# A two-block transformer kernel: weight splits begun at projection steps only, key rotation behind its tile, norm broadcasts behind the projection

## The reference, cut to what matters

```
block 1:  xn = rmsnorm(x)
          q_a,k_a,v_a, q_b,f_b,i_b,og_b, g_a,g_b = split(xn @ w_in)      # 9 x 1024 columns
          y_a = attention(rope(q_a), rope(k_a), v_a; 16 heads of 64, causal) @ w_br_attn
          y_b = hgrn2(q_b, f_b, i_b, og_b; 8 heads of 128, norm per head) @ w_br_hgrn
          h = x + (sigmoid(g_a)*y_a + sigmoid(g_b)*y_b) @ w_out
          h = h + cross_attention(rmsnorm(h), rmsnorm(mem); 4 heads of 256) @ wo
          h = h + (silu(u)*v) @ w_ffn_out,  u,v = split(rmsnorm(h) @ w_ffn_in)  # hidden 2816
          x = rmsnorm(h)
block 2, layer 0 (adaLN from c; 512 tokens, 8 heads):
          q,k,v,z = split(h @ a_w_in);  q,k = rope(q), rope(k)           # image tokens only
          o = softmax(q1 k1) v - lam * softmax(q2 k2) v
          o = rmsnorm(o, subln_g) per head * (1 - lam_init)
          x = x + gate * rmsnorm((o * silu(z)) @ w_out)
block 2, layer 1: grouped-query attention (8 query, 2 key heads of 128), norm of q and k, rope,
          the same frame
```

## Time and profile before

| | before |
|---|---|
| median of 3 runs (lowest to highest) | 1512.51 us (1512.04 to 1514.78) |
| profiled execution: its own time | 1509.61 us |
| its span, first to last instruction | 1507.8 us |
| TensorE (PE) busy | 1281.3 us, 85% |
| PE weight load busy (beside PE) | 1118.7 us, 74% |
| VectorE (DVE) busy | 809.2 us, 54% |
| ScalarE (ACT) busy | 591.9 us, 39% |
| GpSimd (POOL) busy | 53.6 us, 4% |
| granted TensorE clock, mean over the span | 0.908 of full |
| DMA | 170.80 MB, 113 GB/s |

### The profile page before, as it was taken

The page is one execution under the profiler, slowest core; times in us unless marked ns, Lnnn a source line. Parts: engine busy times, 40 slices in busy tenths (PEclk is TensorE's granted clock), DMA queues, the critical chain, the costliest instruction groups (busy, mean ns, idle before and its releaser), DMA issues.

```text
span 1507.8 us, 22059 instructions
## 1 busy us (share of the span) xinstructions
PE 1281.3 (85%) x8336; PEld 1118.7 (74%) x8336; DVE 809.2 (54%) x1600; ACT 591.9 (39%) x1053; POOL 53.6 (4%) x57
## 2 busy tenths in 40 slices
PE   3899998987966798999999989988888779696886
PEld 3899887887965797988888877765555557585485
DVE  3565544558736855555664435554454352654653
ACT  3674345342221243433333334544433233343442
POOL 0000000002112000000000000000000000010000
PEclk9899999998987899999999979999888879588998
DMA  5254443332211252387846711121111012022020
GB/s 227 95 177 155 141 141 112 126 126 85 98 70 56 99 188 81 130 303 286 310 172 232 273 42 67 61 70 42 42 42 42 28 42 84 28 71 70 1 85 29
DMA packets 46809, 170.80 MB, mean 113 GB/s; under 512 B 5200, under 2 KB 5840, under 8 KB 46064
## 3 DMA queue, kind: packets, MB, share of 16 engines
q1 hardware_dynamic: 46080, 165.58, 31.2%
q0 software_dynamic: 624, 3.80, 0.7%
HBM read 168.31 MB, written 1.05 MB: 112 GB/s over the span
## 4 chain that ended last, share of the span: by engine, by line
PE 62%; issue 16%; DVE 12%; ACT 4%; POOL 0%; ACTq 0%; DVEq 0%; POOLq 0%
PE lin L1003 14%; PE lin L1004 13%; PE lin L1005 13%; PE sum_bank L1059 4%; PE lin L1017 3%; PE lin L1019 2%; PE lin L1018 2%; DVE w_lo L1400 2%; PE o_bank L1114 2%; PE sum_bank L1072 2%; PE score L1092 2%; ACT w_hi L1218 2%; PE score L1137 1%; PE score L1035 1%; DVE stat L1634 1%
## 5 line engine op out<-in xcount | busy, mean ns | idle before, releaser
L1400 DVE TENSOR_TENSOR w_lo<-w_raw,w_hi 128x1024 fp32r<-128x1024 f32 (+1 forms) x264 | 319.6, 1213 | 358.1 <-ACT w_hi L1218 305.6
L1218 ACT CAST w_hi<-w_raw 128x1024 fp32r<-128x1024 f32 (+1 forms) x264 | 270.7, 1037 | 160.5 <-PE lin L1005 128.7
L1003 PE MATMUL lin<-XH,w_hi 128*128 128x256 f32 x448 | 134.2, 299 | 1.1 <-DVE w_lo L1400 0.7
L1004 PE MATMUL lin<-XL,w_hi 128*128 128x256 f32 x448 | 131.4, 293 | 0.0
L1005 PE MATMUL lin<-XH,w_lo 128*128 128x256 f32 x448 | 131.1, 293 | 0.0
L1059 PEld LDWEIGHTS sum_bank<-ones,sqr 128*128 128x128 f32 x528 | 84.5, 237 | 57.4 <-ACT sqr L1247 42.4
L1059 PE MATMUL sum_bank<-ones,sqr 128*128 128x2 f32 x528 | 84.1, 277 | 45.1 <-ACT sqr L1247 38.5
L1003 PE MATMUL lin<-NH,w_hi 128*128 128x256 f32 x416 | 120.3, 289 | 0.0
L1004 PE MATMUL lin<-NL,w_hi 128*128 128x256 f32 x416 | 117.6, 283 | 0.0
L1005 PE MATMUL lin<-NH,w_lo 128*128 128x256 f32 x416 | 117.6, 283 | 0.0
L1335 ACT ACTIVATE probs<-score,stat 128x512 f32<-128x512 f32 (+1 forms) x88 | 52.9, 606 | 115.4 <-DVE stat L1639 94.9
(11 more groups left out here) (322 smaller groups left out, 3090.8 us busy)
## 6 DMA issues: line engine op xcount, KB each, us to landing
w_raw<-in_ada SPq DMA_DIRECT2D x48, 512.0 KB, 5.7
w_raw<-in_w_out SPq DMA_DIRECT2D x24, 512.0 KB, 3.2
w_raw<-in_gate SPq DMA_DIRECT2D x22, 512.0 KB, 6.2
w_raw<-in_up SPq DMA_DIRECT2D x22, 512.0 KB, 3.7
w_raw<-in_ffn_out SPq DMA_DIRECT2D x16, 512.0 KB, 3.8
w_raw<-in_q SPq DMA_DIRECT2D x16, 512.0 KB, 3.3
w_raw<-in_z SPq DMA_DIRECT2D x16, 512.0 KB, 3.2
w_raw<-in_k SPq DMA_DIRECT2D x10, 512.0 KB, 3.2
```

The lines of the kernel that those rows point to most:

```text
L1003: nc.tensor.matmul(bank[:, 0:W], wh, moving(H, kk), start=first, stop=False)
L1004: nc.tensor.matmul(bank[:, 0:W], wh, moving(L, kk), start=False, stop=False)
L1218: scal.copy(w_hi[:, i % HL, 0:n], raw[:, tile["i"] % RAW, 0:n]).then_inc(w_hi_ready, 1)
L1400: vec.tensor_sub(w_lo[:, i % HL, 0:n], raw[:, tile["i"] % RAW, 0:n], w_hi[:, i % HL, 0:n].bitcast(F32)).then_inc(w_lo_ready, 1)
```

## The change

Two edits.

The first is in `split`'s calls. At every step that is not a projection, ACT and DVE now call it with a reach that is one tile shorter. That is the reach that the last projection step already had, so at these steps nothing new is issued any more: every split is issued at the head of a projection step, ahead of the eviction of that step's own tile, and tile pos+2 is the furthest one.

The second is in `fill_da`, the weaving of the differential attention. The rotation of the next head's K moves from part 1 into part 0, directly behind the projection that makes K. The broadcast and application of the norm of head h-2 (`sub_apply`) moves from ahead of that projection to behind it and behind the rotation.

```diff
@@ fill_da
             h, part = divmod(fills[0], 3)
             fills[0] += 1
-            if part == 0 and h >= 2:
-                sub_apply(h - 2)
-            elif part == 1 and h >= 1:
+            if part == 1 and h >= 1:
                 sub_norm(h - 1)
             elif part == 2 and h >= 1:
                 rt_step(sub[h - 1])
@@
             if part == 0 and nxt < DA_HEADS:
                 rope_2(Q2, nxt)
                 wide_2("k_2", nxt, K2)
-            elif part == 1 and nxt < DA_HEADS:
                 rope_2(K2, nxt)
                 roped_2.append(n_rope[0])
+            elif part == 1 and nxt < DA_HEADS:
                 if h < 3:
                     values_2(2 * h + 2)
                 else:
@@
             elif len(z_early) < 7:
                 gate_early(len(z_early))
+            if part == 0 and h >= 2:
+                sub_apply(h - 2)
@@ the walk of ACT, and the same lines in the walk of DVE
                 else:
-                    split(pos + LOOK, stream)
+                    split(pos + LOOK - 1, stream)
```

## The result

The changed kernel takes 1445.66 us in the median of 4 runs (1445.15 to 1446.65), the kernel before, run beside it, 1512.28 in the median of 4: a ratio of 0.9563 with a 95% interval of 0.9540 to 0.9586. The direction was right, the size was not.

A forecast was written before the change was run, and what follows sets the result against it. It took PE's order of work to set the end, with about 226 us of PE standing still, often behind early weight splits. Terms -9.4, -7.8, -10.7, -12.4, -7.8, -0.6 gave -48.7, so about 1463 us, range 1447 to 1488.

The forecast's parts named there:

- the clock: Half-speed loss in the differential attention heads taken as unchanged (0); 3.4 us saved behind its first round.
- a new wait: Heads h = 2 to 6: PE waits 4.4 us for diag behind K's rotation, +22.0; 7 to 10 us half speed each.
- The attention of block 1: Block 1 attention: w_lo no longer ahead of AH and AL, sum -7.8; -8.8 with its output.
- more than forecast: the clock: Whole kernel, rival: about 1440 us, because with short gaps gone the clock stays full; chance 0.09.
- The heads' waits: Differential attention heads: diag waits -11.8, waits for rotated K -16.5, new broadcast waits +22.0; net -6.3 us.
- The attribution: Heads: moving K's rotation and the norm broadcast removes waits of 11.8 and 16.5 us and adds 22.0.
- The start: Kernel start: lamt and diag ready earlier, -11.1, one later v-tile split, +1.7; sum -9.4 us.
- HGRN: HGRN stage: four places lose a w_lo or w_hi ahead of needed work; sum -10.7 us, -9.7 in the stage table.
- The 0.6 at the residual projections: Elsewhere in block 1's tail: -0.6 us.
- Starvation: Projections, rival: shorter lead makes weight tiles late, 104 us in 46 fills, about 1565 us; chance 0.05.
- the change does nothing: Whole kernel, rival: PE's 62% of the chain holds all of it, 1512 us; chance 0.03.

The follow-up runs named there:

- The filler run: Changed kernel plus 16 unread 128x128 by 128-column matmuls in each of the five broadcasts that wait for diag; measured 1435.7 us, ratio 0.949.
- the first experiment: Edit 1 alone (the splits' shorter reach on both engines), weaving of the differential attention as in the kernel before; measured 1407.6 us, ratio 0.930.

## Why the prediction was wrong

In the main, the waits went and came where the prediction put them; what failed is one term, the clock, and one attribution. By size, 22.3 us of clock were missing from the sum and 7.3 us of waits were too many, so a part of the error cancelled.

**The clock, the step that failed.** For the heads it said "17 to 25. I take 0", and outside them it booked 3.4 us in all. Measured: PE busy fell by 25.7 us with the same matmuls, and the waits by 38.0 where 45 were forecast. Of the 25.7, the heads gave 10.0 in place of the 0. (1 - 0.91) x 250.4 = 23 us were lost there before, (1 - 0.94) x 228 = 14 now. Clock windows, columns as in the earlier trace rows, first of the kernel before, behind a wait of 1.91 us for diag and behind one of 4.11 for K:

```profile
1018.10:1025.00 6.90, 6.90 (x30) 5.25 (x30) 2.62 (x5) 2.02 (x6) 0.00 (x0) 1.00 0.00 0
1072.70:1081.20 8.50, 8.50 (x23) 6.02 (x24) 4.68 (x13) 2.24 (x6) 1.01 (x1) 0.50 0.18 64
```

and of the changed kernel, behind its new waits of 4.28 and 4.37 us:

```profile
958.70:964.70 6.00, 6.00 (x19) 3.71 (x20) 3.76 (x9) 0.59 (x1) 0.00 (x0) 0.50 0.00 0
1030.20:1033.10 2.90, 2.90 (x8) 1.43 (x8) 0.77 (x2) 0.00 (x0) 0.00 (x0) 0.50 0.00 0
1033.20:1040.00 6.80, 6.80 (x35) 5.41 (x36) 4.51 (x13) 3.44 (x11) 0.00 (x0) 1.00 0.00 0
```

The mis-sized price is that of a new wait: 7 to 10 us at half speed each, 17 to 25 lost in five. Two of the five had 6.8 us and three 3.4, which is 12 lost, some 10 of them while PE worked. The four old waits for K had 6.8 or 10.2 us, 17 lost; two of the six old diag waits had 3.4 us each behind them, which the prediction did not count, and four had none. Why one wait of 4.1 to 4.4 us is followed by 3.4 us at half speed and another by 10.2 stays open. The filler run shows what all five cost: 9 to 10 us. Outside the heads I counted each short gap at its own length and no more; with them went half speed that I did not book, 15.7 us of PE's busy time against the 3.4. The attention of block 1 shows it: 8.2 us of waits went, near the 8.8 forecast, and 5.2 of busy time besides. The rival "more than forecast: the clock" was the nearest to what happened, and it had a chance of 0.09. Of what the prediction cites from the Trainium skill, "TensorE: Matmul & The Clock Gate", section "HAM oscillation — how this bites in real kernels", that idle gaps between bursts throttle the clock again, the trace agrees with the direction: behind each new wait of 4.3 us the clock was at half (0.50 in the window from 958.70).

**The heads' waits.** Those taken off and those put on came out as priced: the new wait was 4.28 to 4.37 against 4.4 forecast, in five heads, and K's 16.5 us and the old diag waits went. The small waits of the values for wideT (4.9 us in eight, now 0.7) and one of 1.1 for the squares went too, which I did not see: waits fell by 12.4 us in the heads (38.0 to 25.6), where 6.3 were forecast.

**The attribution.** The sum gave edit 2 the removal of 28 us of waits and charged it 22, a gain of 6. In truth edit 1 removes them by itself, and edit 2 costs 38 us. The forecast of the whole did not need this, so no number of it shows the mistake; the first experiment does. The question I did not ask at 1033.32 was why the instructions ahead of the rotation were so late.

**Smaller ones.** The start (-9.4 against -9.2) and HGRN (-9.7 against -8.4) came out in size, in part by luck: the waits that went are 6.7 and 5.3 us, and unbooked clock made up 2.5 and 3.1. The 0.6 at the residual projections was wrong in sign: +6.8, since there the split moves from behind an eviction to ahead of it. I had looked at what the split leaves, not at what it now stands ahead of. Starvation did not come: waits of the projections for w_lo rose from 6.9 to 8.7 us in all (2.4 the longest), a little over the 8 that the prediction allowed and far from its 50, and "the change does nothing" fell with the result.

## What to carry to other kernels

In a program that every engine walks in order, preparatory work that can wait (here a split that needs another engine's half) belongs where what it waits for is already done; one instruction that stands waiting on DVE delays the whole chain behind it, and the engine that is blamed in the waits may stand three links further on. Ask of each wait why its releaser was late before moving the releaser: here one shorter reach took away both kinds of wait, and the reordering made for one of them cost 38 us. And when gaps of TensorE are removed or added, give the stretch at half clock behind them a term of its own, beside the gaps' length: here it was 25.7 us beside 38.0.

## What the runs showed of the hardware

In the changed kernel half clock came with a wait of 4.3 us of PE in all five cases, for 3.4 or 6.8 us; in the kernel before, with the four waits of 4.1 us, for 6.8 or 10.2 us, and behind two of the six waits of 1.9 to 2.3 us, for 3.4. In the changed kernel, keeping PE busy in the wait with products that nobody reads took it away and gave 10 us back, though the time to diag itself stayed. Over the program, PE's busy time fell by 25.7 us beside 38.0 us of waits.
